# Recurrent-gate products of a two-layer block as three fp32r passes over split operands

## The chip, the core and the metric

The program runs on one core of one Trainium2 chip. Its time is the device time of one execution in microseconds; the figure used is the median of several executions. The core has TensorE (PE in the profile; its weight loads are PEld), VectorE (DVE), ScalarE (ACT), GpSimd (POOL) and SyncE (SP), which issues the transfers. Each engine works through its own instructions in order and waits on semaphores for the others.

## The reference, cut to what matters

A sequence of 256 tokens with 2048 features goes through a first block (attention, state-space mixer, cross attention, MLP) and a second, hybrid layer. The second layer multiplies the input by a large matrix, cuts the result into ten parts, and puts the part `xr` through a causal convolution and a gated linear recurrence (RG-LRU). Its gates are block-diagonal: 16 blocks of 128 features, each with two 128x128 weight matrices.

```python
xr = causal_dwconv(xr, rnn_conv_w, rnn_conv_b)
def rg_lru(x, w_a, b_a, w_i, b_i, lam):
    xb = x.reshape(B, T, RNN_BLOCKS, RNN_BLOCK)            # 16 blocks of 128
    r = jax.nn.sigmoid(jnp.einsum('btnc,ncd->btnd', xb, w_a) + b_a).reshape(B, T, D_RNN)
    i = jax.nn.sigmoid(jnp.einsum('btnc,ncd->btnd', xb, w_i) + b_i).reshape(B, T, D_RNN)
    log_a = -LRU_C * r.astype(jnp.float32) * jax.nn.softplus(-lam.astype(jnp.float32))
    a = jnp.exp(log_a)
    mult = jnp.sqrt(-jnp.expm1(2.0 * log_a))
    u = mult * (i * x).astype(jnp.float32)
    _, h = lax.associative_scan(combine, (a, u), axis=1)   # h[t] = a[t] h[t-1] + u[t]
```

The change is about the two `einsum` lines: 32 products of a 128x128 matrix with a 128x256 block.

## The kernel before, in words

All large products are made of "grans": one gran is 256 rows by 512 columns of a weight matrix (512 KB). For each gran g, SyncE loads the fp32 weights into the ring `raw` (5 buffers); ScalarE's `high(g)` rounds them to fp32r in `WH` (4 slots, line 1399); VectorE's `low(g)` writes the remainder into `WL` (line 2005); TensorE multiplies in three passes, high by high, high by low and low by high (line 903), 24 matmuls of 256 columns. ScalarE may overwrite a slot of the ring only when TensorE has finished the gran four before.

A plan, made when the program is built, gives every gran a time slot and puts every other step into a slot, the first one in which it is allowed and in which enough buffers are free. Each engine then walks through the slots and issues, within a slot, its steps in an order that is written out at the end of its function. In slot t TensorE multiplies the gran of slot t, VectorE splits the gran of slot t+2 and ScalarE that of t+3; each of them does this split ahead of the other steps of its slot. The slots are no clock: an engine goes on to its next instruction as soon as its semaphores allow.

The part `xr` is four chunks of eight grans. A chunk gives two units u (an even one and an odd one), each of two blocks n = 2u and 2u+1. If E is the slot of a chunk's last gran, the even unit goes through `xr_tap` (ScalarE, E+1), `xr_taps` (VectorE, the convolution, E+2), `lru_pe` (TensorE, the gates' products, E+4), `lru_tanh` (ScalarE, E+5), `lru_la` (VectorE, E+6), `lru_exp` (ScalarE, E+7), `lru_m` (VectorE, E+8), `lru_sqrt` (ScalarE, E+9, which is E+1 of the next chunk) and `lru_scan` (VectorE, E+10, which is E+2 of the next chunk). The odd unit runs one slot behind. In a slot TensorE does its gran first, then `lru_pe`. The gates' weights lie in `lw`, four blocks deep, loaded by SyncE once `lru_pe` has freed a block; `lru_pe` multiplies plain fp32 operands, and the profile counts two records for each such matmul.

Of the kernel before, what the change touches and what calls it, by code (L numbers as in the profile page):

```python
# [7 lines left out]
F32 = mybir.dt.float32  # L8
F32R = mybir.dt.float32r
I32 = mybir.dt.int32  # L10
ALU = mybir.AluOpType
ACT = mybir.ActivationFunctionType
# [30 lines left out]
def col_layout():  # L43
# [19 lines left out]
    "dn": "xbc_scale", "kw_ki": "dt_acs", "rq": "ssm_gain", "lru_la": "ssm_rs",  # L63
    "lru_m": "rope_angle", "lru_scan": "rope_sin", "tk_start": "rope_cos", "gt_taps": "xr_taps", "ln_lo": "mg_lo",
    "res_stat": "ln_stat", "res_y": "lam_end", "res_p": "ln_acc", "res_bn": "add3",
    "res_copy": "ln_fin", "res_z": "gt_tap",
    "add3": "dn", "ln_yw": "rq",

# [279 lines left out]
def make_plan():  # L348
    P = Plan()
    E, T, B = P.end, P.T, P.B  # L350
# [15 lines left out]
    for u in range(8):  # L366
        t = max(E("xbc", u // 2) + 1, rs + 1) + u % 2
# [14 lines left out]
    for j in range(8):  # L382
        t = E("qkqk"[j // 2], j // 4) + 1 + 2 * (j % 2)
# [9 lines left out]
    t = max(xs + 1, z0 + 1)  # L393
    for u in range(8):
        t = max(t, (z0, z0 + 1, z - 1, z)[u // 2] + 1)
# [3 lines left out]
        t = P.chain(t, u, ("ssd_spread", "ssd_exp", "ssd_mask", "ssd_y", "ssd_out"), *bufs) - 1  # L399
# [6 lines left out]
    out, sq = [], []  # L406
    for u in range(8):
        out.append(head_steps(P, u, rope[3] + 1 + 4 * u if u < 4 else rope[7] + 1))
    for u in range(4):
        t = max(out[2 * u + 1], E("v", 1)) + 1  # L410
# [7 lines left out]
    for u in range(8):  # L418
        t = P.chain(max(E("w_out_a", u // 2) + 1, row + 1) + u % 2, u, ("adda",), (T, ("adda", u), "adda", "adda"))
# [3 lines left out]
    m = max(E("w_out_s", 3) + 2, out[7] + 2)  # L423
# [62 lines left out]
        done = t  # L486
    for u in range(8):
        t = P.chain(E("xr", u // 2) + 1 + u % 2, u, ("xr_tap", "xr_taps"))
        steps = ("lru_pe", "lru_tanh", "lru_la", "lru_exp", "lru_m", "lru_sqrt", "lru_scan")
        t = P.chain(t + 2, u, steps, (B, ("lru", 2 * u), "lru_pe", "lru_tanh"), (B, ("lru", 2 * u + 1), "lru_pe", "lru_tanh"),  # L490
                    (T, ("lru_g", 2 * u), "lru_tanh", "lru_m"), (T, ("lru_g", 2 * u + 1), "lru_tanh", "lru_m"),
                    (T, ("lru_y", 2 * u), "lru_la", "lru_scan"), (T, ("lru_y", 2 * u + 1), "lru_la", "lru_scan"))
        hh.append(t)
    t = mask + 1
    for h in range(16):
# [80 lines left out]
def flat(x):  # L576
    return x.rearrange("p a t -> p (a t)")
# [6 lines left out]
def f32(x):  # L584
    return x.bitcast(F32)


def program(nc, A):
# [4 lines left out]
    with ctx:  # L593
        def sb(name, shape, dt=F32, stack=ctx):
            return stack.enter_context(nc.sbuf_tensor(name, shape, dt))
# [50 lines left out]
            cv = sb("cv", [128, 2, 512], F32, p2)  # L646

        with ExitStack() as p3:
            qi = sb("qi", [128, 8, 256], F32, p3)
            ki = sb("ki", [128, 256], F32, p3)  # L650
            wi = sb("wi", [128, 32], F32, p3)
            k2 = sb("k2", [128, 4, 256], F32, p3)
            v2 = sb("v2", [128, 2, 512], F32, p3)
            q2 = sb("q2", [128, 16, 256], F32, p3)
            xr = sb("xr", [128, 16, 256], F32, p3)
            lw = sb("lw", [128, 4, 2, 128], F32, p3)
            score = sb("score", [128, 384], F32, p3)
            work = sb("work", [128, 384], F32, p3)
            mbias = sb("mbias", [128, 384], F32, p3)
            c4 = sb("c4", [128, 16], F32, p3)  # L660
            sps = sb("sps", [128, 4, 16], F32, p3)
            tab = sb("tab", [128, 4, 256], F32, p3)

        with ExitStack() as p4:
            AH4 = sb("AH4", [128, 16, 256], F32R, p4)
# [14 lines left out]
        def pair(x, u):  # L680
            return flat(x[:, 2 * u:2 * u + 2, :])
# [8 lines left out]
        def S(*key):  # L690
            return ps[4 + P.B.of[key]]
# [205 lines left out]
        def tensor(e):  # L897
# [4 lines left out]
            def mm(out, l, r, start=True):  # L902
                return e.matmul(out, l, r, start=start, stop=True, skip_group_check=True)  # L903
# [372 lines left out]


            def lru_pe(u):
                for n in (2 * u, 2 * u + 1):
                    out = S("lru", n)  # L1280
                    on.wait_ge(*s("xr_taps", u + 1))
                    on.wait_ge(s[f"lw{n % 4}"], 16 * (n // 4 + 1))
                    free_S(on, "lru", n)
                    mm(out[:, 0:256], lw[:, n % 4, 0, :], xr[:, n, :])
                    mm(out[:, 256:512], lw[:, n % 4, 1, :], xr[:, n, :]).then_inc(s["lru_pe"], 1)


            def ln_mean(_):
# [105 lines left out]
        def scalar(e):  # L1394
# [268 lines left out]
            def xr_tap(u):  # L1663
# [5 lines left out]
                           bias=V("rnn_b", f))  # L1669
                m.then_inc(s["xr_tap"], 1)  # L1670

            def lru_tanh(u):
                for n in (2 * u, 2 * u + 1):
                    y, x = T("lru_g", n), S("lru", n)
                    free_T(on, "lru_g", n)
                    on.wait_ge(*s("lru_pe", n + 1))
                    fn(y[:, 0:256], x[:, 0:256], ACT.Tanh, scale=0.5, bias=V("lru_ba", n))
                    m = fn(y[:, 256:512], x[:, 256:512], ACT.Tanh, scale=0.5, bias=V("lru_bi", n))
                m.then_inc(s["lru_tanh"], 1)
# [140 lines left out]
            for t in range(P.slots):  # L1820
# [42 lines left out]
                    lru_exp(u)  # L1863
                for u in P("lru_tanh", t):
                    lru_tanh(u)
                for u in P("v2_copy", t):
                    v2_copy(u)
                for u in P("ix_relu", t):
# [72 lines left out]
        def gpsimd(e):  # L1941
            on = Waits(e)
            own = Tick(s["pool"])

            def add(out, a, b):
                return e.tensor_tensor(out, a, b, ALU.add)  # L1946

            def norm_add(n, u):
                acc = T("norm", n, 0)
                if u > 1:  # L1950
                    on.wait_ge(*s(f"norm_add{n}", u - 1))
                if u == NORM_PAIRS[n]:
                    m = add(acc[:, 0:256], acc[:, 0:256], acc[:, 256:512])
                else:
                    on.wait_ge(*s(f"norm_sq{n}", u + 1))
                    m = add(acc[:, :], acc[:, :], T("norm", n, u)[:, :])
                m.then_inc(s[f"norm_add{n}"], 1)

            def ln_acc(u):
                x, q = T("ln_x"), T("ln_sq", 0)  # L1960
                if u > 1:
                    on.wait_ge(*s("ln_acc", u - 1))
                if u == 6:
                    add(x[:, 0:256], x[:, 0:256], x[:, 256:512])
                    add(q[:, 0:256], q[:, 0:256], q[:, 256:512]).then_inc(s["ln_acc"], 1)
                    return
                on.wait_ge(*s("ln_sq", u + 1))
                if u == 1:
                    free_T(on, "ln_x")
                add(x[:, :], pair(xT, 0) if u == 1 else x[:, :], pair(xT, u))  # L1970
                add(q[:, :], q[:, :], T("ln_sq", u)[:, :]).then_inc(s["ln_acc"], 1)

            def ln_sub(u):
                y = two(T("ln_y", u))
                on.wait_ge(*s("ln_meanrow", 1))
                on.wait_ge(*s("ln_yw", P.nth["ln_yw", u]))
                e.tensor_tensor(y, y, twice(rb[:, 3, :]), ALU.add).then_inc(s["ln_sub"], 1)

            def res_p(t, c):
                x = res_part(t, c)  # L1980
                on.wait_ge(s["rows"], 16)
                on.wait_ge(*s("res_z", P.nth["res_z", (t, c)]))
                e.tensor_tensor(x, x, res_row(0, c), ALU.mult).then_inc(*own.up())
                on.wait_ge(*own.now)
                add(x, x, res_row(1, c)).then_inc(s["res_p"], 1)

            e.memset(small[:, :], 0.0).then_inc(s["zero"], 1)
            for t in range(P.slots):
                for n in range(1, 5):
                    for u in P(f"norm_add{n}", t):  # L1990
                        norm_add(n, u)
                for u in P("ln_acc", t):
                    ln_acc(u)
                for u in P("ln_yw", t):
                    ln_sub(u)
                for i, c in P("res_p", t):
                    res_p(i, c)


        def vector(e):  # L2000
# [3 lines left out]
            def tt(out, a, b, op):  # L2004
                return e.tensor_tensor(out, a, b, op)  # L2005
# [552 lines left out]
            def xr_taps(u):  # L2558
# [2 lines left out]
                later_taps(halves_of(bank("xr", u // 2, u % 2)), [xr[:, 2 * u + k, :] for k in range(2)],  # L2561
                           taps).then_inc(s["xr_taps"], 1)

            def lru_la(u):
                on.wait_ge(*s("lru_tanh", u + 1))
                on.wait_ge(*s("lam_end", 1))
                for n in (2 * u, 2 * u + 1):
                    g, y = T("lru_g", n), T("lru_y", n)
                    free_T(on, "lru_y", n)
                    ts(y[:, 0:256], g[:, 0:256], 1.0, c4[:, n:n + 1], ALU.add, ALU.mult)  # L2570
                    m = stt(xr[:, n, :], g[:, 256:512], 1.0, xr[:, n, :], ALU.add, ALU.mult)
                m.then_inc(s["lru_la"], 1)
# [203 lines left out]
            for t in range(P.slots):  # L2776
# [55 lines left out]
                    lru_m(u)  # L2832
                for u in P("lru_la", t):
                    lru_la(u)
                for u in P("rq", t):
                    rq(u)
                for u in P("tk_mask", t):
# [238 lines left out]
```

## Time and profile before

| | |
|---|---|
| median of 3 executions | 2631.86 us (2631.58 to 2631.89) |
| the profiled execution's own time | 2631.25 us |
| its span in the profile | 2629.5 us |
| PE busy | 2606.2 us, 99% of the span |
| DVE busy | 1747.2 us, 66% |
| ACT busy | 1330.6 us, 51% |
| POOL busy | 80.2 us, 3% |

The span is the stretch from the first to the last instruction of the profiled execution; its own time is 1.75 us longer. Busy PE includes the tail of each matmul, which overlaps the next one, so the cost of a matmul is the distance between two starts (its pitch), not its duration. DVE's and ACT's shares are means over stages with very different loads.

### The profile page before, as it was taken

How to read it: one execution, taken by the hardware profiler on the slowest of the kernel's cores; microseconds unless marked ns; L12 is line 12 of the kernel's file. 1: busy time of each engine (PE TensorE's matmuls, PEld its weight loads, DVE VectorE, ACT ScalarE, POOL GpSimd, SP SyncE). 2: the span in 40 equal slices, each digit the busy share in tenths (PEclk: the TensorE clock that was granted, in tenths of full speed). 3: DMA queues.
4: the chain of work that ended last, by engine and by line, in shares of the span. 5: the costliest groups of instructions: out<-in, count | busy, mean ns of one | idle time of the engine just before them, and what ended most of it. 6: DMA issues, size and time to landing. Idle time of an engine off the chain costs nothing.

```text
span 2629.5 us, 50625 instructions
## 1 busy us (share of the span) xinstructions
PE 2606.2 (99%) x21444; PEld 2528.1 (96%) x21444; DVE 1747.2 (66%) x2547; ACT 1330.6 (51%) x1803; POOL 80.2 (3%) x57
## 2 busy tenths in 40 slices
PE   9999999999999999999999999999999999999997
PEld 9987898999999999999899999999999999999996
DVE  7787788765555555556786786556676656665665
ACT  6474675644443443444445774444555435543553
POOL 0000021100000000000000000000400000000001
PEclk9999999999999999999999999999999999999999
DMA  7545556566666666665554556665465665566653
GB/s 259 180 150 166 187 161 200 161 207 194 193 193 194 194 196 194 193 194 185 168 166 150 167 193 194 195 195 179 153 204 196 194 225 193 193 195 195 195 187 118
DMA packets 137170, 490.15 MB, mean 186 GB/s; under 512 B 15344, under 2 KB 17904, under 8 KB 136816
## 3 DMA queue, kind: packets, MB, share of 16 engines
q1 hardware_dynamic: 136224, 485.87, 58.7%
q8 instruction: 168, 2.75, 0.4%
q10 hardware_dynamic: 720, 1.06, 0.1%
q14 instruction: 58, 0.48, 0.1%
HBM read 484.77 MB, written 2.10 MB: 185 GB/s over the span
## 4 chain that ended last, share of the span: by engine, by line
PE 95%; DVE 4%; ACT 1%; issue 0%; DMA 0%; ACTq 0%; DVEq 0%
PE ps L903 94%; DVE WL L2005 1%; PE ps L906 1%; DVE XL L2013 1%; ACT WH L1399 0%; DVE xg L2005 0%; DVE stat L2013 0%; DVE XL L2005 0%; DVE T L2005 0%; DVE xg L2013 0%; DVE T L2013 0%; DVE small L2013 0%; DMA xg<-in_xg 0%; ACT P L1399 0%; PE ps L1013 0%
## 5 line engine op out<-in xcount | busy, mean ns | idle before, releaser
L2005 DVE TENSOR_TENSOR WL<-raw,WH 128x1024 fp32r<-128x1024 f32 (+1 forms) x911 | 1116.6, 1229 | 778.9 <-ACT WH L1399 778.6
L1399 ACT ACTIVATE WH<-raw 128x1024 fp32r<-128x1024 f32 (+1 forms) x911 | 962.0, 1057 | 1239.0 <-PE ps L903 1237.4
L903 PE MATMUL ps<-XH,WH 128*128 128x256 f32 (+1 forms) x4704 | 1307.3, 278 | 5.0 <-DVE WL L2005 2.0
L903 PE MATMUL ps<-XL,WH 128*128 128x256 f32 (+1 forms) x4704 | 1300.0, 276 | 0.0
L903 PE MATMUL ps<-XH,WL 128*128 128x256 f32 (+1 forms) x4704 | 1299.9, 276 | 0.0
L903 PEld LDWEIGHTS ps<-XH,WH 128*128 128x128 f32 (+1 forms) x4704 | 881.8, 187 | 10.0 <-issue 6.7
L903 PEld LDWEIGHTS ps<-XL,WH 128*128 128x128 f32 (+1 forms) x4704 | 881.8, 187 | 0.8
L903 PEld LDWEIGHTS ps<-XH,WL 128*128 128x128 f32 (+1 forms) x4704 | 881.7, 187 | 0.3
L903 PE MATMUL ps<-AH,WH 128*128 128x256 f32 x1600 | 441.8, 276 | 0.0
L903 PE MATMUL ps<-AL,WH 128*128 128x256 f32 x1600 | 441.6, 276 | 0.0
L903 PE MATMUL ps<-AH,WL 128*128 128x256 f32 x1600 | 441.6, 276 | 0.0
L903 PEld LDWEIGHTS ps<-AH,WH 128*128 128x128 f32 x1600 | 300.3, 188 | 0.0
L903 PEld LDWEIGHTS ps<-AL,WH 128*128 128x128 f32 x1600 | 300.3, 188 | 0.0
L903 PEld LDWEIGHTS ps<-AH,WL 128*128 128x128 f32 x1600 | 300.3, 188 | 0.0
L903 PE MATMUL ps<-WH,XH 128*128 128x512 f32 x256 | 103.5, 404 | 0.0
L903 PE MATMUL ps<-WL,XH 128*128 128x512 f32 x256 | 100.4, 392 | 0.0
L903 PE MATMUL ps<-WH,XL 128*128 128x512 f32 x256 | 100.0, 391 | 0.0
L2013 DVE SCALAR_TENSOR_TENSOR T<-ps,cols,T 128x254 f32<-128x254 f32 (+2 forms) x180 | 74.1, 473 | 0.0
L1946 POOL TENSOR_TENSOR T<-T 128x512 f32<-128x512 f32 (+1 forms) x35 | 52.3, 1497 | 482.8 <-ACT T L1399 482.1
L903 PE MATMUL ps<-WH,AH 128*128 128x512 f32 x160 | 63.7, 398 | 0.3 <-DVE AL L2005 0.3
L903 PE MATMUL ps<-WL,AH 128*128 128x512 f32 x160 | 62.8, 392 | 0.0
L903 PE MATMUL ps<-WH,AL 128*128 128x512 f32 x160 | 62.3, 390 | 0.0
(246 smaller groups left out, 1733.6 us busy)
## 6 DMA issues: line engine op xcount, KB each, us to landing
raw<-in_w_up SPq DMA_DIRECT2D x304, 512.0 KB, 4.3
raw<-in_w_in SPq DMA_DIRECT2D x222, 512.0 KB, 3.7
raw<-in_w_down SPq DMA_DIRECT2D x216, 512.0 KB, 4.1
raw<-in_w_out SPq DMA_DIRECT2D x64, 512.0 KB, 4.2
raw<-in_w_gates SPq DMA_DIRECT2D x64, 512.0 KB, 4.3
raw<-in_w_ckv SPq DMA_DIRECT2D x16, 512.0 KB, 3.7
raw<-in_w_cq SPq DMA_DIRECT2D x8, 512.0 KB, 4.4
raw<-in_w_co SPq DMA_DIRECT2D x8, 512.0 KB, 3.7
```

The lines of the kernel that those rows point to most:

```text
L903: return e.matmul(out, l, r, start=start, stop=True, skip_group_check=True)
L906: return e.transpose(out, x, C("ident")[0:n, 0:n])
L1399: return e.activation(out, x, func, **kw)
L1946: return e.tensor_tensor(out, a, b, ALU.add)
L2005: return e.tensor_tensor(out, a, b, op)
L2013: return e.scalar_tensor_tensor(out=out, in0=a, scalar=x, in1=b, op0=op0, op1=op1)
```

## The change

The gates' products are no longer made from fp32 operands but, as everywhere else, from operands split into a high and a low fp32r part, in three passes. Two units' worth of split operands fit (`r = u % 2`): `xrh` and `xrl` for the input, `lwh` and `lwl` for the weights. They lie in memory that the indexer (`qi`, `ki`, `wi`, `score`, `work`) has left by then. The even unit's `lru_hi` stands in slot E+3 and its `lru_lo` in slot E+4; the weights' low part is GpSimd's (`lru_wl`), in E+3. All steps that were there before keep their slots, and so does `lru_pe`.

```diff
-        steps = ("lru_pe", "lru_tanh", "lru_la", "lru_exp", "lru_m", "lru_sqrt", "lru_scan")
-        t = P.chain(t + 2, u, steps, (B, ("lru", 2 * u), "lru_pe", "lru_tanh"), (B, ("lru", 2 * u + 1), "lru_pe", "lru_tanh"),
+        steps = ("lru_hi", "lru_lo", "lru_pe", "lru_tanh", "lru_la", "lru_exp", "lru_m", "lru_sqrt", "lru_scan")
+        t = P.chain(t + 1, u, steps, (B, ("lru", 2 * u), "lru_pe", "lru_tanh"), (B, ("lru", 2 * u + 1), "lru_pe", "lru_tanh"),
...
+        P.put("lru_wl", u, t - steps[::-1].index("lru_lo"))
...
             def lru_pe(u):
+                r = u % 2
+                on.wait_ge(*s("lru_wl", u + 1))
+                on.wait_ge(*s("lru_lo", u + 1))
                 for n in (2 * u, 2 * u + 1):
-                    out = S("lru", n)
-                    on.wait_ge(*s("xr_taps", u + 1))
-                    on.wait_ge(s[f"lw{n % 4}"], 16 * (n // 4 + 1))
+                    k = n % 2
                     free_S(on, "lru", n)
-                    mm(out[:, 0:256], lw[:, n % 4, 0, :], xr[:, n, :])
-                    mm(out[:, 256:512], lw[:, n % 4, 1, :], xr[:, n, :]).then_inc(s["lru_pe"], 1)
+                    for g in range(2):
+                        out = S("lru", n)[:, 256 * g:256 * g + 256]
+                        a = 256 * k + 128 * g
+                        h, l = lwh[:, r, a:a + 128], lwl[:, r, a:a + 128]
+                        mm(out, h, xrh[:, r, k, :])
+                        mm(out, h, xrl[:, r, k, :], False)
+                        m = mm(out, l, xrh[:, r, k, :], False)
+                    m.then_inc(s["lru_pe"], 1)
...
+            def lru_hi(u):
...
+                for n in (2 * u, 2 * u + 1):
+                    on.wait_ge(s[f"lw{n % 4}"], 16 * (n // 4 + 1))
+                fn(lwh[:, r, :], lw[:, 2 * r:2 * r + 2, :, :].rearrange("p n g c -> p (n g c)"),
+                   ACT.Copy).then_inc(s["lru_hi"], 1)
+                on.wait_ge(*s("xr_taps", u + 1))
+                fn(flat(xrh[:, r, :, :]), pair(xr, u), ACT.Copy).then_inc(s["lru_hi"], 1)
...
+            def lru_wl(u):
...
+                on.wait_ge(*s("lru_hi", 2 * u + 1))
+                e.tensor_tensor(lwl[:, r, :], w, f32(lwh[:, r, :]), ALU.subtract).then_inc(s["lru_wl"], 1)
...
+            def lru_lo(u):
+                r = u % 2
+                on.wait_ge(*s("lru_hi", 2 * u + 2))
+                tt(flat(xrl[:, r, :, :]), pair(xr, u), f32(flat(xrh[:, r, :, :])), ALU.subtract).then_inc(s["lru_lo"], 1)
```

TensorE, the products of the first unit, before (`ps` is the PSUM bank; XH, XL, WH, WL are a gran's operands):

```order
L903 MATMUL ps<-XH,WL 128x256
L903 MATMUL ps<-xr,lw 128x256 [waits s_lw0,s_xbc_taps]
L903 MATMUL ps<-xr,lw 128x256
L903 MATMUL ps<-xr,lw 128x256 [waits s_lw1]
L903 MATMUL ps<-xr,lw 128x256
L903 MATMUL ps<-XH,WH 128x256 [waits s_lo]
```

And now, at the same place between the same two grans (`s_ca_lo` counts `lru_lo`, `s_norm_add4` counts `lru_wl`):

```order
L911 MATMUL ps<-XH,WL 128x256
L911 MATMUL ps<-xrh,lwh 128x256 [waits s_ca_lo,s_norm_add4]
L911 MATMUL ps<-xrl,lwh 128x256
L911 MATMUL ps<-xrh,lwl 128x256
L911 MATMUL ps<-xrh,lwh 128x256
L911 MATMUL ps<-xrl,lwh 128x256
L911 MATMUL ps<-xrh,lwl 128x256
L911 MATMUL ps<-xrh,lwh 128x256
L911 MATMUL ps<-xrl,lwh 128x256
L911 MATMUL ps<-xrh,lwl 128x256
L911 MATMUL ps<-xrh,lwh 128x256
```

The excerpt ends two matmuls before the group does: four fp32 matmuls have become twelve fp32r ones, and the group waits for VectorE's and GpSimd's low parts instead of the convolution and the load.

VectorE now, from the second unit's convolution in slot E+3 of a later chunk to the splits of slots E+4, E+5 and E+6 (L2634 is `lru_scan`, which comes out as SCALAR_TENSOR_TENSOR here; before, the same rows stand without the two of `xrl`):

```order
L2045 TENSOR_TENSOR WL<-raw,WH 128x4x256 [waits s_hi]
L2053 SCALAR_TENSOR_TENSOR xr<-ps,cols,xr 128x255 [waits s_xbc_tap]
L2053 SCALAR_TENSOR_TENSOR xr<-ps,cols,xr 128x255
L2053 SCALAR_TENSOR_TENSOR xr<-ps,cols,xr 128x254 [waits s_dve] x2
L2053 SCALAR_TENSOR_TENSOR xr<-ps,cols,xr 128x253 [waits s_dve] x2
L2045 TENSOR_TENSOR T<-xr,T 128x256 [waits s_rope_cos_act]
L2045 TENSOR_TENSOR T<-xr,T 128x256
L2634 SCALAR_TENSOR_TENSOR xr<-T 128x256 [waits s_dve]
L2634 SCALAR_TENSOR_TENSOR xr<-T 128x256
L2045 TENSOR_TENSOR WL<-raw,WH 128x4x256 [waits s_hi]
L2045 TENSOR_TENSOR xrl<-xr,xrh 128x512 [waits s_ca_hi]
L2045 TENSOR_TENSOR WL<-raw,WH 128x4x256 [waits s_hi]
```

The first `xrl` is the even unit's. It stands behind both convolutions, the preceding chunk's two scans and the split of gran E+6.

ScalarE now, slots E+3 and E+4 of the same chunk (before: the three `WH` rows follow each other directly):

```order
L1414 ACTIVATE WH<-raw 128x4x256 [waits s_gemm,s_raw4]
L1414 ACTIVATE lwh<-lw 128x512 [waits s_lw1,s_lw0]
L1414 ACTIVATE xrh<-xr 128x512 [waits s_xbc_taps]
L1414 ACTIVATE WH<-raw 128x4x256 [waits s_gemm,s_raw0]
L1414 ACTIVATE lwh<-lw 128x512 [waits s_lw3,s_lw2]
L1414 ACTIVATE xrh<-xr 128x512 [waits s_xbc_taps]
L1414 ACTIVATE WH<-raw 128x4x256 [waits s_gemm,s_raw1]
```

Two copies of 128x512 stand between each pair of `high` steps; GpSimd's eight `lru_wl` stand alone in its queue.

## Rows read from the trace of the kernel before

**Rows 1.** The page, busy time by engine and the chain that ended last.

```profile
PE 2606.2 (99%) x21444; PEld 2528.1 (96%) x21444; DVE 1747.2 (66%) x2547; ACT 1330.6 (51%) x1803; POOL 80.2 (3%) x57
...
PE 95%; DVE 4%; ACT 1%; issue 0%; DMA 0%; ACTq 0%; DVEq 0%
```

**Rows 2.** Tile xr: line, engine, operation, count: shortest/median/longest ns, first to last start.

```profile
L903 PE MATMUL ps<-xr,lw x64: 378/379/379, 1458.9 to 1541.0; 128*128 128x256 f32 x64
...
L1399 ACT ACTIVATE XH<-xr x8: 610/613/615, 1771.0 to 1798.2; 128x512 fp32r<-128x512 f32 x8
L2013 DVE SCALAR_TENSOR_TENSOR XL<-xr,XH x8: 681/684/686, 1772.3 to 1799.5; 128x512 fp32r<-128x512 f32 x8
```

**Rows 3.** PE in order of time at 1509 us: start, duration, instruction.

```profile
1509.53 0.28 PE L903 MATMUL ps<-XH,WL 128*128 128x256 f32 x1
1509.65 1.89 PE L903 MATMUL ps<-xr,lw 128*128 128x256 f32 x8
...
1511.49 0.28 PE L903 MATMUL ps<-XL,WH 128*128 128x256 f32 x1
```

**Rows 4.** PE in order of time, the even units' groups of three other chunks.

```profile
1458.94 1.89 PE L903 MATMUL ps<-xr,lw 128*128 128x256 f32 x8
...
1484.29 1.89 PE L903 MATMUL ps<-xr,lw 128*128 128x256 f32 x8
...
1535.00 1.89 PE L903 MATMUL ps<-xr,lw 128*128 128x256 f32 x8
```

**Rows 5.** DVE in order of time before 1509.65, with the idle time before each.

```profile
1500.26 1.23 DVE L2005 TENSOR_TENSOR WL<-raw,WH 128x1024 fp32r<-128x1024 f32 x1 [0.19 <-ACT WH L1399]
...
1506.84 2.42 DVE L2013 SCALAR_TENSOR_TENSOR xr<-ps,cols,xr 128x255 f32<-128x255 f32 x6
1509.18 0.75 DVE L2005 TENSOR_TENSOR T<-xr,T 128x256 f32<-128x256 f32 x2
1509.96 1.27 DVE L2589 TENSOR_TENSOR_SCAN xr<-T 128x256 f32<-128x256 f32 x2
1511.15 3.47 DVE L2005 TENSOR_TENSOR WL<-raw,WH 128x1024 fp32r<-128x1024 f32 x3
```

**Rows 6.** ACT in order of time in the same stretch.

```profile
1493.58 1.06 ACT L1399 ACTIVATE WH<-raw 128x1024 fp32r<-128x1024 f32 x1 [2.02 <-PE ps L903]
...
1505.54 1.05 ACT L1399 ACTIVATE WH<-raw 128x1024 fp32r<-128x1024 f32 x1
1507.18 1.06 ACT L1399 ACTIVATE WH<-raw 128x1024 fp32r<-128x1024 f32 x1 [0.59 <-PE ps L903]
```

**Rows 7.** The first chunk: ACT in slot E+3, DVE in slot E+4.

```profile
1453.76 1.07 ACT L1399 ACTIVATE WH<-raw 128x1024 fp32r<-128x1024 f32 x1 [0.75 <-PE ps L903]
...
1455.61 1.21 DVE L2005 TENSOR_TENSOR WL<-raw,WH 128x1024 fp32r<-128x1024 f32 x1
```

**Rows 8.** POOL and DVE in order of time at 328 us.

```profile
328.30 2.25 POOL L1946 TENSOR_TENSOR T<-T 128x512 f32<-128x512 f32 x1 [8.61 <-ACT T L1399]
332.11 1.28 POOL L1946 TENSOR_TENSOR T<-T 128x512 f32<-128x512 f32 x1 [1.55 <-ACT T L1399]
...
329.32 0.68 DVE L2005 TENSOR_TENSOR xg<-xg,ps 128x512 f32<-128x512 f32 x1
329.96 1.68 DVE L2005 TENSOR_TENSOR WL<-raw,WH 128x1024 fp32r<-128x1024 f32 x1
```

**Rows 9.** PE's last matmul, granted clock (0.86) near 2617.5, first matmuls.

```profile
2614.11 0.39 PE L903 MATMUL ps<-WL,AH 128*128 128x512 f32 x1
...
2617.00:2618.00 1.00, 0.00 (x0) 0.00 (x0) 0.93 (x3) 0.00 (x0) 0.92 (x2) 0.86 0.55 215
...
5.95 0.55 PE L903 MATMUL ps<-XH,WH 128*128 128x256 f32 x1 [1.07 <-DVE WL L2005]
...
9.50 0.41 PE L903 MATMUL ps<-XL,WH 128*128 128x256 f32 x1
9.72 0.39 PE L903 MATMUL ps<-XH,WL 128*128 128x256 f32 x1
```

More of the change, by code:

```diff
@@ L65 @@
     "res_stat": "ln_stat", "res_y": "lam_end", "res_p": "ln_acc", "res_bn": "add3",
+    "lru_hi": "ca_hi", "lru_lo": "ca_lo", "lru_wl": "norm_add4",
     "res_copy": "ln_fin", "res_z": "gt_tap",
@@ L648, in program @@
         with ExitStack() as p3:
-            qi = sb("qi", [128, 8, 256], F32, p3)
-            ki = sb("ki", [128, 256], F32, p3)
-            wi = sb("wi", [128, 32], F32, p3)
             k2 = sb("k2", [128, 4, 256], F32, p3)
@@ L656, in program @@
             lw = sb("lw", [128, 4, 2, 128], F32, p3)
-            score = sb("score", [128, 384], F32, p3)
-            work = sb("work", [128, 384], F32, p3)
             mbias = sb("mbias", [128, 384], F32, p3)
@@ L662, in program @@
             tab = sb("tab", [128, 4, 256], F32, p3)
+            with ExitStack() as p3a:
+                qi = sb("qi", [128, 8, 256], F32, p3a)
+                ki = sb("ki", [128, 256], F32, p3a)
+                wi = sb("wi", [128, 32], F32, p3a)
+                score = sb("score", [128, 384], F32, p3a)
+                work = sb("work", [128, 384], F32, p3a)
+            with ExitStack() as p3b:
+                xrh = sb("xrh", [128, 2, 2, 256], F32R, p3b)
+                xrl = sb("xrl", [128, 2, 2, 256], F32R, p3b)
+                lwh = sb("lwh", [128, 2, 512], F32R, p3b)
+                lwl = sb("lwl", [128, 2, 512], F32R, p3b)
         with ExitStack() as p4:
@@ L1670, in xr_tap @@
                 m.then_inc(s["xr_tap"], 1)
+            def lru_hi(u):
+                r = u % 2
+                if u == 0:
+                    on.wait_ge(*s("ix_qk", 8))
+                    on.wait_ge(*s("tk_mask", 1))
+                elif u > 1:
+                    on.wait_ge(*s("lru_pe", 2 * u - 2))
+                for n in (2 * u, 2 * u + 1):
[4 more added lines that the diff above has]
+                fn(flat(xrh[:, r, :, :]), pair(xr, u), ACT.Copy).then_inc(s["lru_hi"], 1)
             def lru_tanh(u):
@@ L1865, in scalar @@
                     lru_tanh(u)
+                for u in P("lru_hi", t):
+                    lru_hi(u)
                 for u in P("v2_copy", t):
@@ L1971, in ln_acc @@
                 add(q[:, :], q[:, :], T("ln_sq", u)[:, :]).then_inc(s["ln_acc"], 1)
+            def lru_wl(u):
+                r = u % 2
+                w = lw[:, 2 * r:2 * r + 2, :, :].rearrange("p n g c -> p (n g c)")
+                on.wait_ge(*s("lru_hi", 2 * u + 1))
+                e.tensor_tensor(lwl[:, r, :], w, f32(lwh[:, r, :]), ALU.subtract).then_inc(s["lru_wl"], 1)
             def ln_sub(u):
@@ L1991, in gpsimd @@
                         norm_add(n, u)
+                for u in P("lru_wl", t):
+                    lru_wl(u)
                 for u in P("ln_acc", t):
@@ L2562, in xr_taps @@
                            taps).then_inc(s["xr_taps"], 1)
+            def lru_lo(u):
+                r = u % 2
+                on.wait_ge(*s("lru_hi", 2 * u + 2))
+                tt(flat(xrl[:, r, :, :]), pair(xr, u), f32(flat(xrh[:, r, :, :])), ALU.subtract).then_inc(s["lru_lo"], 1)
             def lru_la(u):
@@ L2834, in vector @@
                     lru_la(u)
+                for u in P("lru_lo", t):
+                    lru_lo(u)
                 for u in P("rq", t):
```

## The prediction

> **What bounds the kernel now.** I read the page first, then TensorE's own instructions where the change sits, then VectorE's and ScalarE's in the same microseconds. The page says that TensorE is busy in 99% of the span and carries 95% of the chain that ended last [rows 1]. So a microsecond of matmul removed is a microsecond gained, and a wait added in front of a matmul is lost in full, since nothing on TensorE can pass it. VectorE's 66% and ScalarE's 51% are means; what matters is how far each is behind at eight places, the groups of `lru_pe`.
>
> TensorE in order of time shows one such group [rows 3]: the last matmul of gran E+4 at 1509.53, the fp32 group at 1509.65, and the second matmul of the next gran at 1511.49. TensorE did not wait. The even units of the other chunks stand at 1458.94, 1484.29 and 1535.00 [rows 4]: from the second on, a chunk takes 25.35 us.
>
> VectorE at that moment is far behind [rows 5]. The split of slot E+3 starts at 1500.26, about when ScalarE delivers, and from there VectorE has no idle time: both convolutions (the second at 1506.84), two products and two scans of the odd unit of the chunk before (1509.18 and 1509.96), and only at 1511.15 the split of gran E+6, its first step of slot E+4. TensorE has then left slot E+4. Before, this lag cost nothing, because the splits have slots to spare and the convolutions were done long before `lru_pe`. ScalarE waits for TensorE at 1493.58, in slot E-1, with 2.02 us idle [rows 6], so the lag is built up anew in each chunk from TensorE's own position and isn't carried over. Everything below rests on that.
>
> **The matmuls.** From 1509.53 to 1511.49 are 1.96 us, and two ordinary matmuls lie in it. With a pitch p a group costs 1.96 - 2p, and a chunk of eight grans of 24 matmuls and two groups is 192p + 2 (1.96 - 2p) = 25.35 [rows 3, 4]: p is 0.114 and a group 1.73 us; the 64 records are eight groups [rows 2, 3]. The new group is twelve fp32r matmuls of the same 256 columns: 12 x 0.114 = 1.37 us. Gain 0.36 us per group, 2.9 us for eight. The bounds: a row of fp32r matmuls can hardly go below the grans' pitch, so the gain is at most 3; if the switch between operands cost one or two more pitches at a group's start, 0.2 us each, the gain would be 1.3. I take 2.9, since the new group has the form of a gran.
>
> **ScalarE.** Sixteen copies of 128x512, 0.613 us each by the nearest form [rows 2], 9.8 us in all, in slots E+3 and E+4. The step `high` of E+3 runs 1505.54 to 1506.6, so `lwh` is ready at about 1507.1 and `xrh` at 1507.7 (the even unit's convolution comes before 1506.84). `high` of E+4, which today starts at 1507.18 [rows 6], starts 0.5 us later; `lwh` of the odd unit is ready at 1509.2 and `xrh` at 1509.9, held by the second convolution, which ends at 1509.26 [rows 5]. The next `high` has to wait for gran E+4 until 1509.65 anyway. So these 9.8 us lie in idle time and cost nothing. Without that cover, if ScalarE were full, they would cost at most 9.8.
>
> **VectorE, the even unit.** This is the large term. `xrl` is queued in slot E+4 behind the split that starts at 1511.15. Three splits take 3.47 us there, a pitch of 1.13; `xrl` has two SBUF inputs of 128x512, as XL<-xr,XH with 0.684 us [rows 2, 5]. It is ready at 1511.15 + 1.13 + 0.68 = 1512.96. TensorE asks for it at 1509.65. It waits 3.3 us, and behind it on TensorE are gran E+5 and all that follows; the weight loads can't replace that. The same in the chunks whose even groups stand today at 1484.29, 1509.65 and 1535.00 [rows 3, 4]: three stalls, 9.9 us.
>
> In the first chunk there are no scans of a chunk before. ScalarE's `high` of E+3 starts at 1453.76, VectorE's split at 1455.61 [rows 7]; `xrl` follows at 1457.4, or at 1458.6 with the delay told of below, and TensorE asks at 1458.94 [rows 4]. No stall, with 0.3 us in hand at the worst.
>
> **VectorE, the odd unit.** Its `xrl` comes one split later, 1.13 + 0.68 after the even one. TensorE has in between the even group (1.37) and gran E+5 (2.72). No stall. After the last `xrl` VectorE is 3 to 4 us late, but so is TensorE; the splits of grans E+6 and E+7 are ready before TensorE comes to them. SyncE's loads into `lw` wait for `lru_pe` and are needed 20 us later: nothing.
>
> **GpSimd.** Eight subtractions of 128x512. Alone such an operation takes 1.28 us, beside VectorE's work 2.25 [rows 8]. The rows at 328 us show how: the GpSimd addition begins at 328.30 and ends at 330.55, while VectorE's operation with a PSUM input goes on undisturbed (0.68), and the split at 329.96, both inputs in SBUF, takes 1.68 instead of 1.22, until GpSimd is through. One of the two waits for the whole operation of the other.
>
> The Trainium skill says the same, in SBUF — State Buffer, section "Who interferes with whom": an operation of VectorE with two SBUF inputs contends with GpSimd operations that read SBUF, one with at most one such input does not. By this rule, and the trace agrees, it matters beside what `lru_wl` runs.
>
> The even unit's runs from 1507.2 beside the convolution, which reads PSUM: no harm. The odd unit's can start at 1509.2 to 1509.5, exactly beside the products and scans of 1509.18 to 1511.15, all SBUF [rows 5]. It takes its turn between two of them, and VectorE loses about 1.25 us in front of the even unit's `xrl`. Bounds: 0 if GpSimd fits beside the convolution; 2 x 1.25 if both units' operations come in between. I take 1.25, so each of the three stalls is 3.3 + 1.25 = 4.55 us, 13.7 us in all. `lwl` itself is ready by 1511, before `xrl`.
>
> **The sum.** -2.9 + 13.7 = +10.8 us. Against the profiled execution's own 2631.25: 2642.05. The median of the runs is 0.61 above that execution, so 2642.7. Its own range is 2638.5 to 2646.
>
> **The rivals.**
>
> *The stall without GpSimd's part* (0.15). VectorE's lag is in the rows, GpSimd's place in it is worked out to 0.3 us. Three stalls of 3.3: -2.9 + 9.9 = +7.0, 2638.9.
>
> *The stalls also lower TensorE's clock* (0.22). After its last matmul (2614.11, end 2614.50) the granted clock of 2617 to 2618 reads 0.86: it went from 2.4 to 1.2 GHz at about 2617.7, after 3.2 us without work [rows 9]. A stall of 4.55 is longer. What comes then is seen at the start of the kernel, where the first grans' matmuls are 0.21 apart from 5.95 to 9.72: some 18 or 19 of them, 0.1 us dearer each, 1.9 us. Three times that is 5.6: 2648.3. Against it: the level need not fall at every stall, and no stall of that length is in this trace with work behind it.
>
> The Trainium skill, TensorE: Matmul & The Clock Gate, section "HAM oscillation — how this bites in real kernels", has this as a rule: a wait between two bursts of matmuls can bring the clock down each time, so that each burst starts slow. By it the time would be near 2648; no row here shows it in midstream.
>
> *Only the gain* (0.04, the other side). If `xrl` were ready by 1509.65, the time would be 2631.9 - 2.9 = 2629.0, not slower. The place is VectorE's queue between 1500.26 and 1511.15, and the point from which it decides is 3.3 us less lag (4.55 with GpSimd). For it speaks only the first chunk, where the same chain fits. Against it: the order keeps the scans ahead of `xrl`, and none of their durations changes.
>
> *The stalls are half hidden* (0.07). Were VectorE's idle time before 1500.26 used up earlier by the shorter groups, a stall might be 1.5 to 2.5 us: 2633 to 2637. I see no row that does this.
>
> The forecast itself has 0.50, and 0.02 stays for worse.
>
> **Range and chances.** What this kernel's measurement can tell from no change is about 0.2%, 5.3 us. Faster by more than that isn't in any case, for the gain is at most 3: 0.01. Within it lie the gain alone and the half hidden stalls: 0.11. The rest, 0.88, is slower. The range goes from 2636.5, just below the stalls without GpSimd, to 2648.5, the lowered clock three times.
>
> **What would show it.** In the changed profile: the wait of PE for DVE `xrl` in the list of waits, three times 4.5 us (3.3 without GpSimd's part), none for the first chunk and none for `lwl`; DVE's products or scans near the odd `lru_wl` longer by about 1.2 us; twelve matmuls at 0.114 where the group was; ACT's `high` steps still waiting for PE in slot E-1. Wrong would be: PE idle before `lwl`, a stall in the odd groups, a granted clock below 1 after a stall, or no wait at all.

## The result and the profile after

The changed kernel takes 2647.14 us (median of 4 runs, 2646.75 to 2647.77) against 2631.84 before: 15.3 us more, ratio 1.0058, 95% interval 1.0046 to 1.007. The range held it, the predicted 2642.7 was 4.4 us short. The profiled execution took 2647.77, 16.5 more than that of before.

TensorE in the changed kernel, in order of time (start, duration, instruction, idle time before it); this is the even group that stood at 1484.29 in [rows 4]:

```profile
1483.56 0.28 PE L911 MATMUL ps<-XH,WL 128*128 128x256 f32 x1
1488.04 0.55 PE L911 MATMUL ps<-xrh,lwh 128*128 128x256 f32 x1 [4.20 <-issue]
1488.38 0.41 PE L911 MATMUL ps<-xrl,lwh 128*128 128x256 f32 x1
1488.60 0.41 PE L911 MATMUL ps<-xrh,lwl 128*128 128x256 f32 x1
...
1493.08 0.38 PE L911 MATMUL ps<-XH,WL 128*128 128x256 f32 x1
1493.29 0.29 PE L911 MATMUL ps<-XH,WH 128*128 128x256 f32 x1
1493.42 0.28 PE L911 MATMUL ps<-XL,WH 128*128 128x256 f32 x1
```

From start to start are 4.48 us where 0.11 is usual: a pause of 4.37. The idle time printed is shorter, 4.20, because the matmul before it has a tail. After the pause the starts are 0.21 apart instead of 0.11 until 1493.1. The list of TensorE's waits sums up the three pauses, and puts them down to no engine:

```profile
PE ps L911 <- issue: 12.6, 3, 4.2
```

"issue" hides the cause here. VectorE's queue shows it (the same stretch as [rows 5], one chunk earlier):

```profile
1480.87 2.42 DVE L2053 SCALAR_TENSOR_TENSOR xr<-ps,cols,xr 128x255 f32<-128x255 f32 x6
1483.21 0.75 DVE L2045 TENSOR_TENSOR T<-xr,T 128x256 f32<-128x256 f32 x2
1483.99 2.23 DVE L2634 TENSOR_TENSOR_SCAN xr<-T 128x256 f32<-128x256 f32 x2
1486.14 1.19 DVE L2045 TENSOR_TENSOR WL<-raw,WH 128x1024 fp32r<-128x1024 f32 x1
1487.26 0.68 DVE L2045 TENSOR_TENSOR xrl<-xr,xrh 128x512 fp32r<-128x512 f32 x1
```

`xrl` ends at 1487.94 and TensorE starts at 1488.04. The two scans take 2.23 instead of 1.27 [rows 5]. GpSimd's two subtractions of this chunk say why:

```profile
1481.22 1.30 POOL L2009 TENSOR_TENSOR lwl<-lw,lwh 128x512 fp32r<-128x512 f32 x1 [21.58 <-ACT lwh L1414]
1483.21 1.88 POOL L2009 TENSOR_TENSOR lwl<-lw,lwh 128x512 fp32r<-128x512 f32 x1 [0.69 <-ACT lwh L1414]
```

The first runs beside the convolution and neither is slowed. The second starts with the products. They keep their 0.75 us, the subtraction takes 1.88 instead of 1.30, and then the scans take 2.23 instead of 1.27. I read this as each waiting for the other in turn; `e4` below tests the part of it that costs time.

The clock, in windows of a microsecond (after the five engines' busy times comes the granted clock as a share of 2.4 GHz):

```profile
1486.00:1487.00 1.00, 0.00 (x0) 0.00 (x0) 1.00 (x2) 0.29 (x1) 0.00 (x0) 0.73 0.00 0
...
1493.00:1494.00 1.00, 1.00 (x9) 1.00 (x8) 0.13 (x1) 0.00 (x0) 0.00 (x0) 0.85 0.90 336
...
1520.00:1521.00 1.00, 1.00 (x10) 1.00 (x9) 1.00 (x2) 0.45 (x2) 0.00 (x0) 0.80 0.71 229
```

In the second chunk it falls to 1.2 GHz at about 1486.5, inside the pause, and comes back at 1493.3. In the third and fourth TensorE resumes at 1519.56 and 1550.24; the clock falls some 1.0 to 1.1 us after that and comes back 3.3 us later.

The first chunk has no pause; its first product starts at the pitch of the gran before:

```profile
1459.01 0.28 PE L911 MATMUL ps<-xrh,lwh 128*128 128x256 f32 x1
1459.13 0.27 PE L911 MATMUL ps<-xrl,lwh 128*128 128x256 f32 x1
...
1460.31 0.28 PE L911 MATMUL ps<-xrh,lwl 128*128 128x256 f32 x1
...
1463.17 0.28 PE L911 MATMUL ps<-xrh,lwh 128*128 128x256 f32 x1
```

Twelve matmuls, 0.118 apart: 1.42 us a group. The odd group starts at 1463.17, so an even group and the gran behind it take 4.16 us here. In the kernel before they took 4.50, from 1458.94 [rows 4] to the odd group of the first chunk:

```profile
1463.44 1.89 PE L903 MATMUL ps<-xr,lw 128*128 128x256 f32 x8
```

So the new group saves 0.34 us. In the other three chunks the same stretch takes 6.65, 5.82 and 5.87 us (1488.04 to 1494.69, 1519.56 to 1525.38, 1550.24 to 1556.11). These are 5.9 us more than three times 4.16: 5.6 for the lowered clock, and 0.09 for the first start behind each pause, which `e3` below shows without a fall of the clock (4.25 us each time). The account of the profiled executions: 3 x 4.37 + 5.9 - 8 x 0.34 = 13.1 + 5.9 - 2.7 = 16.3, measured 16.5.

### The profile page after: what moved, and what is told of

Read it like the earlier page. It is cut to its first block, busy times and chain, and to the rows that moved or that the text cites. A ratio compares the mean times of both kernels' runs of the same rounds, so it can differ in the third digit from the quotient of the medians.

```text
span 2646.0 us, 50732 instructions
## 1 busy us (share of the span) xinstructions
PE 2610.3 (99%) x21476; PEld 2532.5 (96%) x21476; DVE 1758.3 (66%) x2555; ACT 1339.5 (51%) x1819; POOL 92.6 (3%) x65
## 4 chain that ended last, share of the span: by engine, by line
PE 93%; DVE 3%; ACT 2%; issue 1%; DMA 0%; POOL 0%; SPq 0%; ACTq 0%; DVEq 0%
PE ps L911 92%; ACT WH L1414 1%; DVE WL L2045 1%; PE ps L914 1%; DVE XL L2053 1%; ACT T L1414 1%; DVE xg L2045 0%; DMA raw<-in_w_in 0%; DVE xg L2053 0%; POOL lwl L2009 0%; DVE T L2045 0%; DVE XL L2045 0%; DVE stat L2053 0%; DVE T L2053 0%; DVE small L2053 0%
## 5 line engine op out<-in xcount | busy, mean ns | idle before, releaser
L1414 ACT ACTIVATE T<-ps 128x512 f32<-128x512 f32 (+2 forms) x122 | 62.3, 541 | 0.1
```

What stands on the lines that cost most here:

```text
L1414: return e.activation(out, x, func, **kw)
```

## The experiments

Each was timed beside the kernel before (medians of 2631.73 to 2631.78). Ratios are against the kernel before, with the 95% interval in brackets.

**The products alone** (`e1`).

```diff
-                        h, l = lwh[:, r, a:a + 128], lwl[:, r, a:a + 128]
-                        mm(out, h, xrh[:, r, k, :])
+                        h, l = XH[:, n, 128 * g:128 * g + 128], XL[:, n, 128 * g:128 * g + 128]
+                        mm(out, h, XH[:, (n + 1) % 16, :])
...
-                for u in P("lru_hi", t):
```

> Leaves out all three splits and multiplies the resident tiles XH and XL instead of the gates' operands; TensorE still does twelve fp32r matmuls per group at the same place, and waits only for the convolution, as before the change. Theory (stall, port, clock): the products by themselves gain; a group costs 12 x 0.118 = 1.41 us against 1.73, so 2631.8 - 8 x 0.32 = 2629.3. Rival (the three passes themselves cost, for instance at the switch of operands): 2632 or more.

Measured: 2629.67 us, ratio 0.9992 (0.9983 to 1.0001), most runs between 2629.1 and 2629.9. The gain is 2.1 us by the medians, with an interval of 2.4 us to either side. The group takes 1.44 from its first start to the next gran's:

```profile
1458.53 0.28 PE L911 MATMUL ps<-XH 128*128 128x256 f32 x1
...
1459.97 0.28 PE L911 MATMUL ps<-XH,WH 128*128 128x256 f32 x1
```

Between the even groups of two chunks lie 24.70 us here (1483.22 to 1532.61 for two) and 25.35 before [rows 4]: 0.33 us for each of the two groups, 2.6 us for eight.

**The splits alone** (`e2`).

```diff
             def lru_pe(u):
-                on.wait_ge(*s("lru_wl", u + 1))
-                on.wait_ge(*s("lru_lo", u + 1))
...
+                    mm(out[:, 0:256], lw[:, n % 4, 0, :], xr[:, n, :])
+                    mm(out[:, 256:512], lw[:, n % 4, 1, :], xr[:, n, :]).then_inc(s["lru_pe"], 1)
```

> Keeps the splits of ScalarE, VectorE and GpSimd where they are, but TensorE multiplies plain fp32 operands as before and doesn't wait for the splits (the reload of the weights, the next splits and the step that overwrites xr wait for them instead). Theory: the splits lie in idle time, 2631.8, and TensorE's groups show no wait; VectorE's scans beside lwl are still 2.2 us for two instead of 1.27. Rival (the added work on ScalarE and VectorE delays the grans' splits, and that is the loss): 2636 or more, with waits of TensorE for WL.

Measured: 2631.76 us against 2631.73, ratio 1.0 (0.9992 to 1.0009). All the added work of ScalarE, VectorE and GpSimd is there, GpSimd's turn included, and costs nothing as long as TensorE doesn't wait for it:

```profile
1484.84 2.23 DVE L2631 TENSOR_TENSOR_SCAN xr<-T 128x256 f32<-128x256 f32 x2
```

In the trace every group starts 0.11 to 0.12 behind the gran before it. So the loss is the wait, neither the work nor the products.

**The pause filled** (`e3`).

```diff
+                if u in (2, 4, 6):
+                    free_S(on, "lru", 2 * u)
+                    for _ in range(9):
+                        mm(S("lru", 2 * u)[:, 0:256], C("ones"), cst[:, CL["ident"][0]:CL["ident"][0] + 256])
                 on.wait_ge(*s("lru_wl", u + 1))
```

> The change, with nine fp32 matmuls of 256 columns of constants (some 3.9 us) in front of the wait of units 2, 4 and 6. They fill the stall and don't lengthen it (4.37 us). Theory: the three stalls stay, but the granted clock stays at 2.4 GHz; the matmuls at 0.213 us pitch after them go, which are worth 2.4 + 1.5 + 1.4 = 5.3 us: 2647.1 - 5.3 = 2641.8. Rival (the lowered clock in the records costs nothing, or comes from something else than the pause): 2647, or the clock falls again.

Measured: 2642.36 us, ratio 1.0042 (1.0029 to 1.0054): 4.8 us below the change. TensorE and the granted clock:

```profile
1483.44 4.04 PE L911 MATMUL ps<-cst 128*128 128x256 f32 x18
1487.86 0.36 PE L911 MATMUL ps<-xrh,lwh 128*128 128x256 f32 x1 [0.37 <-DVE xrl L2049]
```

```profile
1480.00:1500.00 20.00, 19.63 (x155) 18.84 (x155) 16.00 (x28) 13.39 (x25) 3.19 (x2) 1.00 0.49 160
```

The group starts as late as before, the clock stays at 2.4 GHz, and now the profile names VectorE's `xrl` as what ended the wait. The lowered clock is thus 4.8 us of the 15.3 by the medians (5.5 by the two profiled executions), and what is left, 10.6, is the forecast's own case (+10.8).

**GpSimd moved away from the scans** (`e4`). Both units' `lwh` in slot E+2, `lwl` behind them.

```diff
-        P.put("lru_wl", u, t - steps[::-1].index("lru_lo"))
+        at = P.nth_slot("lru_hi", u) - (2 if u % 2 else 1)
+        P.put("lru_wh", u, at)
+        P.put("lru_wl", u, at)
...
```

> The weights' high parts are made earlier, both units' in slot E+2, so that GpSimd's two subtractions run for the most part beside VectorE's convolutions, which read PSUM. Theory: the scans of VectorE go back from 2.23 us to near 1.27 for two, the stall from 4.37 to between 3.4 and 3.8 us, so 3 x 0.6 to 1.0 = 2 to 3 us less, and more if the shorter pause spares some of the lowered clock: 2640 to 2645. Rival (GpSimd's port has no part in the stall): 2647.1.

Measured: 2642.84 us, ratio 1.0043 (1.003 to 1.0055): 4.3 us below the change. The scans are back at 1.27, the pause is 3.45 (3.28 idle and the tail), 0.92 shorter three times, 2.8 us:

```profile
1483.86 1.27 DVE L2643 TENSOR_TENSOR_SCAN xr<-T 128x256 f32<-128x256 f32 x2
```

```profile
1486.95 0.36 PE L916 MATMUL ps<-xrh,lwh 128*128 128x256 f32 x1 [3.28 <-issue]
```

The other 1.5 us are one fall of the clock less: it falls in two of the three chunks here.

**The products a slot later** (`e5`), so that the group and all that follows it come one gran later.

```diff
-                    ... (T, ("lru_y", 2 * u + 1), "lru_la", "lru_scan"))
-        P.put("lru_wl", u, t - steps[::-1].index("lru_lo"))
+                    ... (T, ("lru_y", 2 * u + 1), "lru_la", "lru_scan"), apart=("lru_pe",))
+        P.put("lru_wl", u, t - steps[::-1].index("lru_lo") - 1)
```

> The groups of TensorE and all that follows them stand one slot later; the splits stay where they are. Theory: TensorE asks 2.72 us later (one gran) for an xrl that is ready at about the same time, so the stall of 4.37 us becomes 1.65, too short to lower the clock: 2629.7 (the products alone) + 3 x 1.65 = 2634.6. Rival (the wait is not for VectorE's place in its queue but moves along with TensorE, or is caused by the group itself): 2642 or more.

Measured: 2644.47 us (2641.1 to 2645.4), ratio 1.0047 (1.0034 to 1.0059). A miss by 10 us. That TensorE waits for the end of `xrl` still fits, but the premise that `xrl` would be ready at the same time was wrong: the slot later also moves the scans of the chunk before, one unit's into slot E+3 and one's into E+4. Both now stand ahead of `xrl`, and GpSimd's two subtractions meet the scans of the first pair and the products of the second:

```profile
1482.40 2.33 DVE L2634 TENSOR_TENSOR_SCAN xr<-T 128x256 f32<-128x256 f32 x2
...
1485.77 1.83 DVE L2045 TENSOR_TENSOR T<-xr,T 128x256 f32<-128x256 f32 x2
...
1488.83 0.67 DVE L2045 TENSOR_TENSOR xrl<-xr,xrh 128x512 fp32r<-128x512 f32 x1
```

`xrl` ends at 1489.5, 1.6 us later than in the change. The pauses are 3.4, 3.4 and 2.3. The profiled execution is the fastest of the five (2641.1), with one fall of the clock; the others are 3.1 to 4.3 us slower, and no trace shows why.

**The low part ahead of the scans** (`e6`).

```diff
                 for u in P("xr_taps", t):
                     xr_taps(u)
+                for u in P("lru_lo", t):
+                    lru_lo(u)
                 for u in P("lru_scan", t):
                     lru_scan(u)
```

`lru_lo` also stands in the slot of `lru_hi`, one earlier.

> VectorE makes the input's low part right after the second convolution, ahead of the products and scans of the chunk before (the even unit's in slot E+3, the odd one's in E+4); nothing is left out. Theory: xrl of the even unit is ready 0.3 us after TensorE asks: three stalls of 0.3, clock untouched, 2629.7 + 1 = 2630.7; if GpSimd's lwl comes first in its turn, 1.3 us more per stall, 2634.6. Rival (the stall is not VectorE's queue): 2642 or more.

Measured: 2631.50 us, ratio 0.9999 (0.999 to 1.0008). One step of VectorE moved takes 15.6 us off the change, and the kernel is back where it was. What is left of the gain's 2.1 us is eaten by two short waits per chunk, the second of which I had not expected; `e9` below shows that it is GpSimd's turn before the odd unit's `xrl`:

```profile
1483.98 0.36 PE L912 MATMUL ps<-xrh,lwh 128*128 128x256 f32 x1 [0.16 <-issue]
1488.66 0.36 PE L912 MATMUL ps<-xrh,lwh 128*128 128x256 f32 x1 [0.28 <-issue]
```

**Weights early, and the low part ahead of the convolution** (`e7`): `e4`, with the loop over `lru_lo` before the one over `xr_taps`.

> As the run with the weights' high parts early, and VectorE makes the input's low part ahead of the second convolution. Theory: no stall is left, 2629.7, as the products alone, 2.1 us below the kernel before. Rival (something else waits once the stall is gone, such as GpSimd's low part or the grans' splits behind a VectorE that now waits for ScalarE's xrh): 2631 or more, with a wait of TensorE before a group or a gran of the chunk.

Measured: 2635.96 us, ratio 1.0015 (1.0006 to 1.0024). A miss; the rival named it. VectorE now waits for ScalarE's `xrh`, then for GpSimd, and everything behind it is late, the odd unit's `xrl` by 1.8 us:

```profile
1482.04 1.70 DVE L2055 TENSOR_TENSOR xrl<-xr,xrh 128x512 fp32r<-128x512 f32 x1 [1.26 <-ACT xrh L1420]
...
1489.10 0.68 DVE L2055 TENSOR_TENSOR xrl<-xr,xrh 128x512 fp32r<-128x512 f32 x1
```

```profile
1489.89 0.36 PE L917 MATMUL ps<-xrh,lwh 128*128 128x256 f32 x1 [1.63 <-issue]
```

Three pauses of 1.8 and three of 0.3 are 6.3 us on the products' 2629.67. The clock holds in all three chunks.

**The pause half filled** (`e8`): `range(5)` instead of `range(9)` in `e3`.

> As the run that fills the pause, with five fp32 matmuls instead of nine, some 2.2 us of work, so that 2.2 us of each stall stay empty. Theory: what lowers the clock is a long pause; one of 2.2 us leaves it at 2.4 GHz, as the pauses of up to 1.3 us in the kernel before do: 2642.4, like the full filling. Rival (any pause of over 2 us in a stretch of dense work lowers it): the clock falls in one to three of the chunks and the time is 2644 to 2648.

Measured: 2646.95 us (2645.6 to 2647.5), ratio 1.0056 (1.0043 to 1.0068). The rival was right: nearly nothing is won. The pauses are 2.25 us, and the clock falls in two of the three chunks of the profiled execution (2645.64, one of the two faster of five), here 0.8 us after the work has resumed:

```profile
1517.16 0.36 PE L911 MATMUL ps<-xrh,lwh 128*128 128x256 f32 x1 [2.09 <-DVE xrl L2049]
```

```profile
1517.00:1518.00 1.00, 0.84 (x7) 0.88 (x8) 1.00 (x2) 0.00 (x0) 0.00 (x0) 0.96 0.57 102
1518.00:1519.00 1.00, 1.00 (x6) 1.00 (x6) 1.00 (x3) 0.82 (x2) 0.00 (x0) 0.50 0.95 373
```

**Both small causes apart and together.** `e9` is `e6` with the weights early, `e10` is `e6` with the scans of the chunk before one slot later, `e11` has all three:

```diff
-        steps = (..., "lru_m", "lru_sqrt", "lru_scan")
+        steps = (..., "lru_m", "lru_sqrt", "lru_gap", "lru_scan")
```

(`lru_gap` is a slot in which no engine does anything for the unit.)

> The run with the low part before the scans, and in addition the weights' high parts early. There two short stalls per chunk are left, 0.3 us before the even group and 0.4 before the odd one; VectorE's scans are blocked once by GpSimd (2.26 us for two) ahead of the odd unit's xrl. Theory: without that block the odd stall goes and the even one stays: 2631.5 - 3 x 0.4 = 2630.3. Rival (GpSimd's turn has no part in it): 2631.5.

> The run with the low part before the scans, and in addition both scans of the chunk before stand one slot later on VectorE, behind the low parts' slots. Theory: xrl of the even unit is ready 1.2 us before TensorE asks, that of the odd unit 0.4 us before; no stall is left and the whole gain of the products shows, 2629.7. Rival (ScalarE's xrh or GpSimd's lwl becomes the last one): a short stall per chunk stays, 2631.

> Both of the above together. Theory: no stall, as the products alone, 2629.7, 0.08% below the kernel before. Rival (ScalarE, with two copies more before the step high of slot E+3, holds up xrh and the grans' splits): 2630.5 or more.

Measured: 2630.35 (ratio 0.9995, 0.9986 to 1.0004), 2629.37 (0.9991, 0.9982 to 1.0) and 2629.03 us (0.9989, 0.998 to 0.9998). All three as expected, within 0.7 us. The traces separate the two causes more sharply than the times. In `e9` the odd groups' wait is gone and the even ones keep theirs (0.45 us from start to start where 0.11 is usual). In `e10` the even groups start on time and the odd ones are 0.14 late, too little for the list of waits:

```profile
1487.65 0.28 PE L912 MATMUL ps<-XH,WL 128*128 128x256 f32 x1
1487.90 0.36 PE L912 MATMUL ps<-xrh,lwh 128*128 128x256 f32 x1
```

GpSimd's turn is what is left there: it lengthens the even unit's `xrl` (0.68 in the change) and the products (0.75) on VectorE, ahead of the odd unit's `xrl`:

```profile
1481.62 1.38 DVE L2046 TENSOR_TENSOR xrl<-xr,xrh 128x512 fp32r<-128x512 f32 x1
1482.92 1.85 DVE L2046 TENSOR_TENSOR T<-xr,T 128x256 f32<-128x256 f32 x2
...
1487.12 0.69 DVE L2046 TENSOR_TENSOR xrl<-xr,xrh 128x512 fp32r<-128x512 f32 x1
```

In `e11` all eight groups start 0.11 behind the gran before them:

```profile
1483.85 0.28 PE L917 MATMUL ps<-XH,WL 128*128 128x256 f32 x1
1483.96 0.28 PE L917 MATMUL ps<-xrh,lwh 128*128 128x256 f32 x1
```

Between the even groups of two chunks lie 25.08 us in `e9`, 24.88 in `e10` and 24.66 in `e11` (25.35 before). `e11` is the best kernel of the study, 2.75 us or 0.1% below the kernel before, and the only one whose interval lies wholly below 1. By their medians alone 2629.03 and 2629.37 can't be told apart.

## Why the prediction was right in its direction and short in its size

- *VectorE's queue.* Right: three pauses, at the even groups of the second to fourth chunk, none in the first, none at the odd groups. `xrl` was forecast 1.13 + 0.68 behind the split at the head of slot E+4, and it stands there. `e2` and `e6` show that the place in the queue is the cause: the same work costs nothing when nobody waits for it, and nearly nothing when it stands before the scans.
- *GpSimd's turn.* Right in kind, a little too large: forecast 1.25 per pause, measured 0.96 in the scans, and 0.92 by the pause of `e4`. The rows fit a subtraction that spends its first part waiting for the products. The pause came out at 4.37 instead of 4.55. It meets the odd unit's subtraction only, as forecast, and the convolution that reads PSUM was not slowed.
- *The matmuls.* The gain was right, though both costs that it is the difference of were too small. The new group takes 1.42 us and not 1.37: the pitch in these groups is 0.118, in the grans 0.114. It is so with other operand tiles too (`e1`), so it isn't the new tiles' place in memory; what makes it was not tried. But the old group cost more than 1.73 as well. In `e11`, where no group waits, a chunk takes 24.66 us against 25.35, which is 0.35 per group and 2.8 for eight, where 2.9 were forecast. The medians give 2.1 (`e1`) and 2.75 (`e11`), too coarse to decide this.
- *ScalarE and SyncE.* Right: `e2` is at 2631.76, and its groups don't wait.
- *The clock.* This is the step that failed. I held a steady clock likelier (0.50) than a lowered one (0.22), since the level need not fall at every pause, and put the 1.9 us per pause into that rival's sum alone. It fell at all three, which by my own list of signs is the forecast being wrong. It cost 4.8 us by the medians (`e3`) and 5.6 in the profiled execution. The rival had priced it at 5.6, too; its case stood at 2648.3. The rows had said it: [rows 9] show a fall 3.2 us after the last matmul, and the forecast pause was 4.55. A pause of that length is longer than the idle time before the only fall that the trace showed, so the rival was the likelier case.
- *The range.* It held 2647.14 only by its upper end, 2648.5, which had been laid on this rival. The forecast's own range, 2638.5 to 2646, did not hold it. What the forecast got right is the sign, the cause and the 10.6 us that are left without the clock (`e3`).

Two expectations of mine fell for one reason (`e5`, `e7`): I took the time at which `xrl` would be ready from a queue that the edit itself changed. A third (`e8`) fell because I took a pause of 2.2 us for too short to lower the clock.

## What to carry to other kernels

Before an engine that is busy all the time is made to wait for a new product, read how far behind the producing engine stands at that place, from its queue in order of time and not from its share of busy time: VectorE was busy 66% of the span, and TensorE still waited 4.4 us for it three times. The cure was the order of VectorE's steps, not less work. And a pause of the matmul engine has a second price, the clock after it; filling half of the pause saved nearly none of it here.

## What the runs showed of the hardware that I had not expected

The clock does not fall only when TensorE stands still. In two of the three chunks after the change it fell 1.0 to 1.1 us after work had resumed, in `e8` twice 0.7 to 0.8 us after. And short pauses suffice. In the profiled executions the clock fell after 3 of 3 pauses of 4.4 us (the change), 2 of 3 of 3.45 (`e4`), 1 of 3 of 2.3 to 3.4 (`e5`), 2 of 3 of 2.25 (`e8`), and none of 3 of 1.8 (`e7`) or 0.5 (`e3`). These counts are of one execution each. The fall soonest after the last matmul is in the fourth chunk of `e4`: TensorE's last matmul before the pause ends at 1541.62, and the window

```profile
1543.00:1544.00 1.00, 0.00 (x0) 0.00 (x0) 1.00 (x2) 1.00 (x1) 0.00 (x0) 0.78 0.00 0
```

puts the fall at about 1543.6, some 1.9 us later, where the forecast had only the 3.2 of [rows 9]. The start of the kernel, by contrast, has its matmuls 0.21 apart (5.95 to 9.72, [rows 9]) although the granted clock reads 1.00 there. So the pitch has to be read beside the granted clock.

GpSimd's subtraction is lengthened as VectorE's operations are: it takes 1.30 us beside the convolution, 1.88 where it starts with the two products (the change), and 2.52 in `e6`, where it starts with `xrl` and the products follow.
